# One hybrid decoder layer: another order in the mixer, and dense sums that leave PSUM between the halves of the experts

## The chip, the cores and the metric

The kernel runs on one core of a Trainium2 chip. The metric is the device time of one execution in microseconds; the time of a kernel is the median of its executions. Before the change three executions took 3759.36, 3754.88 and 3768.76 us, so the median is 3759.36.

## The reference, cut to what matters

One layer, `h <- LN(alpha*h + f(h))` three times, over 1024 positions of width 1024, all float32:

```python
# 1. mixer: one projection of h, then two groups of heads side by side
#    GLA: 4 heads, gated linear attention with a decay per channel
scores = einsum('bhtd,bhsd,bhtsd->bhts', qi, ki, decay)
o = scores @ v + (q * exp(b)) @ state;   state = exp(b_last) * state + k_end^T @ v
#    SSD (Mamba-2): 16 heads of width 64, causal convolution, chunked scan with a decay per head
y = (cb * lmat) @ xdt + exp(a_cum) * (c @ h_prev) + d_skip * xs
h = LN(alpha * h + concat(rms(o) * silu(r), rms(y * silu(z))) @ w_out)
# 2. cross-attention, 4 heads, into 256 memory tokens
# 3. PEER: 8 heads x top-16 of 128 x 128 experts of one neuron each
act = einsum('bthk,btd->bthk', u[expert], h)      # u, v: (16384, 1024)
out = einsum('bthk,bthkd->btd', gates * gelu(act), v[expert])
```

## The kernel before, in words

The 1024 tokens are eight tiles of 128. The program has three stages, one after the other; each engine has its own list of instructions in the order of the code and waits on semaphores.

**First stage** (`project_inputs`). Float32 products are made of three products of rounded parts (high x high, high x low, low x high). x comes in eight blocks of 128x1024. For each, VectorE makes the high part (a cast, line 582) and then the low part (a subtraction, line 584); TensorE takes block after block behind them (`product`, line 416). Meanwhile GpSimd cuts the weights (lines 360 to 395), and ScalarE has nothing to do until its first copy (line 493).

**Mixer** (`mix_tokens`). One body per tile on every engine; in the steady part it is a loop of two tiles. TensorE has four PSUM areas A to D of 128x1024, which all products share (`place`). Per tile, in its order: turn x (X, area A), turn the keys (KB, D), level products of heads 0, 1 and 2 (L0 to L2, each eight products of 128x128), turn y of the tile before (OTb, D), L3, the product CB, turn o of the tile before (OTa, B), the products of keys and v (SN), the products with the state (O, line 962), a quarter of the output projection of the tile before (line 895), the diagonal products YD (line 970), and the rest of the projection with YO and HN between. For each head VectorE masks the level products (line 1217) and GpSimd adds the eight levels up in three halvings (lines 864 and 867), 512, 256 and 128 wide; `att_ready` counts heads. The masked terms of heads 0 and 3 share a buffer (`masked`); those of 1 and 2 stand where xdt and xend come later, so these two products (lines 1222 and 1226) wait for their heads' sums. Then VectorE makes the exponents of the next tile's levels (lines 157 to 160), ScalarE exponentiates them (lines 168 to 171) and the SSD decays (line 1098), VectorE multiplies decay by CB (line 1232), and after the root from ScalarE (line 1081) it scales o and updates the state. The output projection's result goes through the first norm on VectorE at the end of the body.

**Retrieval** (`attend_and_retrieve`). Six tiles are gathered, two are dense. The gathered tiles run through 768 slots, one pick of every token each. In a slot GpSimd gathers a row of u per token (`gather_u`, line 1622) and, 20 slots behind (LAG), a row of v (`gather_v`, line 1639), 128 rows of 4 KB each. VectorE multiplies the u rows by h2 and sums (`dot`, line 2180), ScalarE makes the gelu and spreads the weights (line 1965), TensorE combines four rows of v at a time (`combine`, line 1674). u has a ring of five, v of eight. For the first 384 slots the attention and the choice of picks of the later tiles run between ("fronts"). h2 of the current tile stands in PSUM (`h2_near`, the upper half of `wide`) up to slot 443, and in SBUF after it.

The two dense tiles (256 tokens) go through all 16384 experts, in two halves of 64 blocks of 128. From slot 384 (`DENSE_AT`) to 752 their work is laid out over ticks, and `tick_slot` says at which slot a tick comes. A half begins with the *spread*: the gates of the picks are made into a table of 64 keys by 256 tokens per partition. A group is eight tokens: VectorE makes three operations on one-hot rows (`hots`, lines 2446 to 2450), TensorE eight small products (`choose`, line 1779), ScalarE a copy into the table (`keep_chosen`, line 2050). There are 32 groups, two in a tick, and a tick has four slots (`SPREAD_PACE`). Hot rows and results have two buffers each. The picks are read from PSUM (`picksT_near`) in the first spread and from their copy in SBUF (`picksT`) in the second, since by then `wide` holds the sums. Then come the blocks: the table's part times gelu of `dense_u` (line 1791) weighs the block of v in `dense_v` (line 1808), which adds over all 128 blocks in `wide` (128x2048). u and v of the blocks are streamed by SP, 512 KB each. At the end `norm3_a` adds the sums to h2.

## Time and profile before

| what | value |
|---|---|
| median of three executions | 3759.36 us |
| the profiled execution's own time | 3736.6 us |
| its span | 3734.8 us |
| TensorE busy, loading weights | 80%, 54% |
| VectorE, ScalarE, GpSimd busy | 62%, 28%, 52% |
| granted TensorE clock, mean | 0.871 |
| DMA, mean over the span | 292 GB/s |

The profiled execution is 23 us shorter than the median. "Busy" leaves out waiting, branching and issuing. A wait is put down to the event that came last by the profile. All times in the rows are microseconds from the start of the span unless marked ns. A TensorE operation on float32 shows as two records, so eight products of 128x64 stand as x16, and one `dot` as two records of line 2180, of which only the one named CUSTOM is counted below.

### The profile page before, as it was taken

What the parts mean: (1) busy time and instruction counts of PE and PEld (TensorE: products, weight loads), DVE (VectorE), ACT (ScalarE), POOL (GpSimd) and SP (SyncE); (2) the same over time, 40 slices, a digit from 0 to 9 for tenths busy, and PEclk for the clock granted to TensorE, in tenths of its full rate; (3) what the DMA queues carried; (4) which work ended last, traced back from release to release, by engine and by line L of the source; (5) the groups of instructions that cost most, each with busy time, mean ns of one, the idle gap of its engine ahead of it and who ended that gap; (6) DMA issues with size and microseconds to landing.
All of it is one profiled execution on the core that took longest, in us unless ns stands there. A gap on an engine that the chain in (4) does not pass through costs nothing.

```text
span 3734.8 us, 40729 instructions
## 1 busy us (share of the span) xinstructions
PE 3002.1 (80%) x14124; PEld 2007.9 (54%) x14124; DVE 2320.8 (62%) x4974; ACT 1047.2 (28%) x2819; POOL 1925.6 (52%) x1704
## 2 busy tenths in 40 slices
PE   8999978989998756656665544689999967999995
PEld 5878865555656323323323212467777645777771
DVE  3350047777217777778867767776666687666655
ACT  2320123342213323334233212222323222232222
POOL 2342213232103566666665666566565577656566
PEclk9999988999999877777777755679999976999996
DMA  3322252222345999899998999899999999999998
GB/s 123 121 89 96 90 214 83 82 87 83 124 199 185 361 362 375 335 373 369 345 358 337 370 384 347 324 356 409 409 409 409 409 342 329 405 410 409 409 409 341
DMA packets 312855, 1089.76 MB, mean 292 GB/s; under 512 B 33232, under 2 KB 56400, under 8 KB 309600
## 3 DMA queue, kind: packets, MB, share of 16 engines
q0 software_dynamic: 221184, 805.40, 56.6%
q1 hardware_dynamic: 91488, 282.04, 19.8%
q8 instruction: 100, 1.64, 0.2%
q14 instruction: 83, 0.68, 0.0%
HBM read 1051.07 MB, written 36.24 MB: 291 GB/s over the span
## 4 chain that ended last, share of the span: by engine, by line
DMA 18%; PE 17%; POOL 15%; DVE 8%; issue 8%; another core or an unknown queue 3%; ACT 1%; POOLq 0%; DVEq 0%; ACTq 0%
DMA arena<-in_u_dram,idx 12%; POOL arena L1639 7%; POOL arena L1622 7%; DMA arena<-in_v_dram,idx_v 5%; PE small L1791 4%; PE acc L1674 4%; DVE arena L2180 3%; PE wide L1808 3%; PE small L1779 1%; PE small L1733 1%; PE wide L1716 1%; ACT gelu_v L1949 1%; DVE arena L2448 0%; PE small L1881 0%
## 5 line engine op out<-in xcount | busy, mean ns | idle before, releaser
L1622 POOL DMA_INDIRECT arena<-in_u_dram,idx x768 | 797.1, 1038 | 617.7 <-DVE act_u L2180 230.3
L1639 POOL DMA_INDIRECT arena<-in_v_dram,idx_v x752 | 816.1, 1085 | 517.9 <-PE acc L1674 201.4
L1674 PE MATMUL acc<-arena 128*32 128x512 f32 x3008 | 507.3, 792 | 407.7 <-DMA arena<-in_v_dram,idx_v 317.2
L2180 DVE CUSTOM_DVE_ANT_0 arena<-arena,h 128x1024 f32<-128x1024 f32 x348 | 424.2, 1224 | 381.7 <-DMA arena<-in_u_dram,idx 369.2
L2180 DVE CUSTOM_DVE_ANT_0 arena<-arena,wide 128x1024 f32<-128x1024 f32 x420 | 508.4, 1217 | 192.8 <-DMA arena<-in_u_dram,idx 135.1
L1674 PEld LDWEIGHTS acc<-arena 128*32 128x32 f32 x3008 | 102.8, 130 | 678.7 <-issue 563.6
L1791 PE MATMUL small<-pwq 128*128 128x256 f32 x2048 | 466.2, 381 | 1.1 <-DMA pwq<-in_uT_dram 1.1
L1791 PEld LDWEIGHTS small<-pwq 128*128 128x128 f32 x2048 | 386.3, 190 | 82.8 <-issue 26.6
L1965 ACT ACTIVATE arena<-comb,w_v 128x32 f32<-128x32 f32 x768 | 199.0, 311 | 358.9 <-remote 195.3
L416 PE MATMUL group<-w_nat_high,x_parts 128*128 128x512 f32 x768 | 238.2, 391 | 3.8 <-ACT arena L549 3.8
L1779 PE MATMUL small<-arena 128*128 128x64 f32 x1024 | 182.2, 358 | 64.0 <-DVE arena L2450 50.8
L2058 ACT ACTIVATE arena<-small 128x256 f32<-128x256 f32 x128 | 49.3, 385 | 653.0 <-PE small L1791 584.4
L1779 PEld LDWEIGHTS small<-arena 128*128 128x128 f32 x1024 | 175.6, 269 | 104.4 <-DVE arena L2450 69.6
L895 PE MATMUL mix_bank<-memory_tables,mixT 128*128 128x512 f32 x512 | 224.0, 593 | 0.0
L1949 ACT ACTIVATE gelu_v<-act_u 32x4 f32<-32x4 f32 x768 | 159.4, 208 | 222.1 <-DVE act_u L2180 157.3
L416 PE MATMUL group<-x_parts,arena_rounded 128*128 128x512 f32 x864 | 206.8, 400 | 15.7 <-DVE x_parts L584 15.7
L416 PEld LDWEIGHTS group<-x_parts,arena_rounded 128*128 128x128 f32 x864 | 165.2, 193 | 57.8 <-issue 10.8
L1808 PE MATMUL wide<-arena_rounded 128*128 128x512 f32 x512 | 181.5, 436 | 0.2 <-DVE pwq_rounded L2466 0.2
L157 DVE TENSOR_TENSOR arena<-arena 128x256 f32<-128x256 f32 x56 | 31.6, 564 | 236.7 <-DMA arena<-scanT_dram 236.7
L416 PEld LDWEIGHTS group<-w_nat_high,x_parts 128*128 128x128 f32 x768 | 144.3, 188 | 34.6 <-issue 4.2
L1808 PE MATMUL wide<-pwq_rounded,arena_rounded 128*128 128x512 f32 x512 | 160.2, 394 | 0.0
L1808 PE MATMUL wide<-arena_rounded,tables_rounded 128*128 128x512 f32 x512 | 159.1, 392 | 0.0
(347 smaller groups left out, 4618.3 us busy)
## 6 DMA issues: line engine op xcount, KB each, us to landing
pwq<-in_uT_dram SPq DMA_DIRECT2D x128, 512.0 KB
pwq<-in_v_dram SPq DMA_DIRECT2D x128, 512.0 KB
arena<-in_w_nat_dram SPq DMA_DIRECT2D x6, 2048.0 KB, 8.6
nat_dram<-stage SPq DMA_DIRECT2D x48, 256.0 KB, 2.1
arena<-in_u_dram,idx POOLq DMA_INDIRECT x768
arena<-in_v_dram,idx_v POOLq DMA_INDIRECT x752
scanT_dram<-stage SPq DMA_DIRECT2D x22, 512.0 KB, 2.9
arena<-in_w_tr_dram SPq DMA_DIRECT2D x18, 512.0 KB, 3.8
```

What stands on the lines that cost most here:

```text
L416: last = pe.matmul(to, stationary(p, k), moving(q, k), start=(k == 0 and n == 0), stop=(k == KC - 1 and n == 2))
L895: last = pe.matmul(place["OUT"][:, c * 512:(c + 1) * 512], mixT[:, k, :], w_out[:, k, c * 512:(c + 1) * 512], start=(k == 0), stop=(k == 2 ...
L1622: pool.indirect_dma_start(out=u_ring[:, g % U_RING, :], out_offset=None, in_=peer_u, in_offset=bass.IndirectOffsetOnAxis(ap=idx[:, t % KEP ...
L1639: pool.indirect_dma_start(out=v_row(g), out_offset=None, in_=peer_v, in_offset=bass.IndirectOffsetOnAxis(ap=idx_v[:, t % KEPT, n:n + 1], a ...
L1674: last = pe.matmul(acc[c * QUAD:(c + 1) * QUAD, half * 512:(half + 1) * 512], spread_row(at), v_row(at)[:, half * 512:(half + 1) * 512], s ...
L1779: last = pe.matmul(small[:, at:at + HALF_KEYS], hot2[:, q % 2, j, :], hot1[:, q % 2, j, :], start=True, stop=True)
L1791: last = pe.matmul(small[:, at:at + DT], uT_ring[:, i % STREAM, k, :], dense_hT[:, k, :], start=(k == 0), stop=(k == KC - 1))
L1808: last = pe.matmul(wide[:, at:at + 512], w, v[:, c * 512:(c + 1) * 512], start=(i == 0 and n == 0), stop=(i == NKEYS - 1 and n == 2))
L1949: last = act.activation(gelu_v[r * QUAD:(r + 1) * QUAD, h % 2, :].rearrange("p (b c) -> p b c", c=SIDE)[:, :, c], act_u[c * QUAD:(c + 1) * ...
L1965: act.activation(spread_row(g), comb[:, :], ACT.Copy, scale=w_v[:, h % 2, j:j + 1]).then_inc(diag_ready, 1)
L2058: act.activation(gelu_d[:, i % WEIGHED, :], small[:, i % 2 * 512:i % 2 * 512 + DT], ACT.Gelu).then_inc(gelu_d_done, 1)
L2180: dve.tensor_tensor_reduce(out=row, in0=row, in1=against, scale=1.0, scalar=0.0, op0=ALU.mult, op1=ALU.add, accum_out=act_u[:, (n // TOPK) ...
```

## The change

- The high parts of x are cast by ScalarE (new semaphore `x_cut`); VectorE keeps the subtractions.
- In the mixer's body TensorE turns y of the tile before (OTb) right behind X, does L0 to L2, and only then turns the keys (KB); SN comes ahead of the turning of o (OTa). ScalarE scales the turned y first, makes the first eight decays, copies the keys, makes the other eight decays, and makes the exponentials of the next tile behind the root for o. VectorE sums the levels of head 3 itself, with one reduction; xdt and xend both come ahead of the exponents and wait for all four heads.
- A tick of the spread has one group and two slots; TensorE chooses a group one tick behind its hot rows, ScalarE keeps it one tick behind that.
- h2 of the dense tiles is turned at slot 361 (`TURN_AT`), the picks at 384 (`PICKS_AT`); ticks begin at slot 386.
- Each half of the experts has sums of its own in `wide`. Between the halves (slot 569) ScalarE copies the first sums into four pieces of SBUF (`empty_wide`), then puts the picks and h2 back into PSUM; groups from the fourth on (`FROM_SBUF`) and the dots of slots 577 to 627 (`BACK_AT`, `BACK_END`) read them there. `norm3_a` adds the pieces.

```diff
-GROUP_TICKS = GROUPS // 2
+GROUP_TICKS = GROUPS
-SPREAD_PACE = 4
+SPREAD_PACE = 2
@@ first stage, ScalarE
-                act.wait_ge(x_split, 2 * KC)
+                for k in range(KC):
+                    act.wait_ge(x_loaded[k], 16)
+                    act.activation(x_h[:, k, :], x_raw[k], ACT.Copy).then_inc(x_cut, 1)
+                act.wait_ge(x_split, KC)
@@ first stage, VectorE
-                    dve.tensor_copy(x_h[:, k, :], x_raw[k]).then_inc(x_split, 1)
-                    dve.wait_ge(x_split, 2 * k + 1)
+                    dve.wait_ge(x_cut, k + 1)
@@ mixer, TensorE
                     if not first(t):
+                        pe.wait_ge(read["HN"], t)
+                        turned(t - 1, "OTb")
                         pe.wait_ge(levels_ready, t)
-                        pe.wait_ge(read["HN"], t)
-                    (five turns into KB)
-                    if not first(t):
                         pe.wait_ge(read["OUT"], t)
                         levels(t, 0)
...
-                    pe.wait_ge(read["KB"], t + 1)
                     if not first(t):
-                        turned(t - 1, "OTb")
+                        pe.wait_ge(read["OTb"], t)
+                    (five turns into KB)
                     pe.wait_ge(read["L0"], t + 1)
                     levels(t, 3)
...
-                    if not first(t):
-                        pe.wait_ge(read["L3"], t + 1)
-                        turned(t - 1, "OTa")
-                        pe.wait_ge(read["OTb"], t)
+                    pe.wait_ge(read["KB"], t + 1)
                     (products into SN)
+                    if not first(t):
+                        pe.wait_ge(read["L3"], t + 1)
+                        turned(t - 1, "OTa")
@@ mixer, VectorE
+                    dve.wait_ge(read[f"L{SUMMED}"], t + 1)
+                    dve.tensor_reduce(att[:, SUMMED, :], level_terms[SUMMED].rearrange("p (l u) -> p u l", u=P),
+                                      AX, ALU.add).then_inc(att_ready, 1)
                     dve.wait_ge(read["X"], t + 1)
-                    dve.wait_ge(att_ready, GLA_BLOCKS * t + 2)
+                    dve.wait_ge(att_ready, GLA_BLOCKS * (t + 1))
                     dve.tensor_tensor(heads(xdt[:, :], 64), heads(xs[:, :], 64), each(1, 64), ALU.mult)
+                    dve.tensor_tensor(heads(xend[:, :], 64), heads(xs[:, :], 64), each(4, 64), ALU.mult)
                     if not final(t):
                         exponents(t + 1)
-                    dve.wait_ge(att_ready, GLA_BLOCKS * t + 3)
-                    dve.tensor_tensor(heads(xend[:, :], 64), heads(xs[:, :], 64), each(4, 64), ALU.mult)
@@ retrieval
+        PICKS_AT = FRONTS_AT + (TILES - 2) * SPAN + STAGE_SLOTS + CHUNK_SLOTS + 1
+        FROM_SBUF = 3
+        TURN_AT = PICKS_AT - CHUNK_SLOTS // 2
+        DENSE_AT = PICKS_AT + 2
+        BACK_AT = tick_slot(HALF_TICKS) + NEAR_AT
+        BACK_END = tick_slot(HALF_TICKS + GROUP_TICKS + 3) - 4
@@ retrieval, TensorE
-                                                 start=(i == 0 and n == 0), stop=(i == NKEYS - 1 and n == 2))
+                                                 start=(i % HALF_KEYS == 0 and n == 0),
+                                                 stop=(i % HALF_KEYS == HALF_KEYS - 1 and n == 2))
-                    if r < GROUP_TICKS:
-                        for q in (2 * r, 2 * r + 1):
-                            choose(b, q)
+                    if 1 <= r <= GROUP_TICKS:
+                        choose(b, r - 1)
@@ retrieval, ScalarE
+                def empty_wide(t):
+                    act.wait_ge(vb_used, HALF_KEYS)
+                    for n, to in enumerate(held):
+                        last = act.activation(to, wide[:, n * HALF_D:(n + 1) * HALF_D], ACT.Copy)
+                    last.then_inc(part_kept, 1)
+                    act.wait_ge(part_kept, 1)
+                    act.activation(picksT_near, picksT, ACT.Copy).then_inc(picksT_ready, 1)
+                    act.wait_ge(h2_loaded, 16 * t)
+                    act.activation(h2_near, h2[:, t % 2, :], ACT.Copy).then_inc(h2_near_ready, 1)
@@ retrieval, VectorE
-                    picks = picksT_near if b == 0 else picksT
+                    picks = picksT if b == 1 and q < FROM_SBUF else picksT_near
+                    if parts:
+                        dve.wait_ge(part_kept, 2)
+                        for n, part in enumerate(parts):
+                            half = y3[:, n * HALF_D:(n + 1) * HALF_D]
+                            last = dve.tensor_tensor(half, half, part, ALU.add)
-                        for q in (2 * r, 2 * r + 1):
-                            hots(b, q)
+                        hots(b, r)
```

## Rows read from the trace of the kernel before

**Rows 1.** The page, part 1: busy us, share of the span, instructions.

```profile
PE 3002.1 (80%) x14124; PEld 2007.9 (54%) x14124; DVE 2320.8 (62%) x4974; ACT 1047.2 (28%) x2819; POOL 1925.6 (52%) x1704
```

**Rows 2.** Stretch, length; busy us of PE, PEld, DVE, ACT, POOL; clock; DMA share, GB/s.

```profile
509.00:925.00 416.00, 350.39 (x1503) 226.57 (x1502) 294.83 (x465) 144.91 (x368) 136.10 (x99) 0.92 0.33 115
...
2301.00:2498.00 197.00, 142.82 (x778) 101.01 (x774) 152.33 (x230) 50.94 (x160) 119.99 (x125) 0.67 0.91 332
2498.00:2982.00 484.00, 464.67 (x2292) 349.18 (x2288) 302.60 (x518) 142.48 (x386) 294.25 (x251) 0.99 1.03 408
2982.00:3183.00 201.00, 151.35 (x802) 105.58 (x798) 154.80 (x233) 47.12 (x158) 156.68 (x125) 0.68 0.94 339
```

**Rows 3.** Groups by line and shape, 0 to 480 us: busy us, mean ns.

```profile
L584 DVE TENSOR_TENSOR x_parts<-arena,x_parts 128x1024 fp32r<-128x1024 f32 x6 | 10.3, 1720 | 0.2
...
L584 DVE TENSOR_TENSOR x_parts<-stage,x_parts 128x1024 fp32r<-128x1024 f32 x2 | 4.5, 2235 | 0.1
...
L521 ACT ACTIVATE arena<-arena 128x1024 f32<-128x1024 f32 x4 | 4.2, 1062 | 0.0
```

**Rows 4.** Timeline, opening: start us, us, engine, operation, [idle before it, releaser].

```profile
5.94 0.69 DVE L582 CAST x_parts<-arena 128x1024 fp32r<-128x1024 f32 x1 [4.90 <-DMA arena<-in_xT_dram]
...
27.23 8.61 PE L416 MATMUL group<-x_parts,arena_rounded 128*128 128x512 f32 x27 [0.21 <-DVE x_parts L584]
```

**Rows 5.** Timeline of TensorE in one tile of the mixer.

```profile
745.98 1.04 PE L916 MATMUL mix_bank<-ident,xsb 128*128 128x128 f32 x8
...
758.54 1.09 PE L883 MATMUL mix_bank<-ident,o_sb 128*128 128x128 f32 x8 [1.47 <-DVE arena L1217]
...
765.94 1.22 PE L962 MATMUL mix_bank<-gla_state,arena 128*128 128x256 f32 x2 [4.58 <-POOL arena L867]
...
777.95 3.68 PE L970 MATMUL mix_bank<-arena 128*128 128x64 f32 x32
```

**Rows 6.** Timeline of VectorE in the same tile.

```profile
759.82 2.27 DVE L1222 TENSOR_TENSOR arena<-arena,scal 128x1024 f32<-128x1024 f32 x1 [1.33 <-POOL arena L867]
765.15 0.43 DVE L157 TENSOR_TENSOR arena<-arena 128x256 f32<-128x256 f32 x1 [3.06 <-DMA arena<-scanT_dram]
...
772.43 1.22 DVE L1226 TENSOR_TENSOR arena<-arena,scal 128x1024 f32<-128x1024 f32 x1
773.56 2.34 DVE L1232 TENSOR_TENSOR arena<-arena,mix_bank 128x1024 f32<-128x1024 f32 x2
779.96 0.18 DVE L1237 RECIPROCAL arena<-arena 128x4 f32<-128x4 f32 x1 [4.05 <-ACT arena L1081]
```

**Rows 7.** Timeline of ScalarE in the same tile.

```profile
763.16 4.78 ACT L1098 ACTIVATE arena<-arena,scal 128x128 f32<-128x128 f32 x16
772.54 3.19 ACT L168 ACTIVATE arena<-arena 128x3584 f32<-128x3584 f32 x1 [4.60 <-DVE arena L160]
...
778.33 1.28 ACT L1081 ACT_TABLE_LOAD   x1
```

**Rows 8.** Timeline of GpSimd in the same tile, last steps of two sums.

```profile
762.75 0.45 POOL L867 TENSOR_TENSOR arena<-arena 128x128 f32<-128x128 f32 x1
...
765.30 0.58 POOL L867 TENSOR_TENSOR arena<-arena 128x128 f32<-128x128 f32 x1
```

**Rows 9.** Busy times by stretch, behind TensorE's wait in that tile.

```profile
766.00:769.00 3.00, 3.00 (x7) 2.46 (x8) 3.00 (x5) 1.94 (x7) 1.90 (x1) 0.50 0.00 0
```

**Rows 10.** Groups by line, first spread, 2301 to 2498 us.

```profile
L1779 PE MATMUL small<-arena 128*128 128x64 f32 x512 | 92.2, 360 | 36.9 <-DVE arena L2450 23.9 <-issue 12.9
...
L1639 POOL DMA_INDIRECT arena<-in_v_dram,idx_v x62 | 59.8, 965 | 47.2 <-PE acc L1674 18.0 <-issue 15.6 <-remote 13.6
...
L2446 DVE TENSOR_TENSOR arena<-iota,wide 128x512 f32<-128x512 f32 x32 | 21.8, 682 | 16.1 <-ACT arena L2043 8.2 <-remote 7.9
```

**Rows 11.** Groups by line, second spread, 2982 to 3183 us.

```profile
L1622 POOL DMA_INDIRECT arena<-in_u_dram,idx x62 | 80.1, 1292 | 21.2 <-issue 18.3 <-DVE act_u L2180 2.9
...
L1639 POOL DMA_INDIRECT arena<-in_v_dram,idx_v x63 | 77.1, 1223 | 24.7 <-issue 17.4 <-PE acc L1674 7.3
```

89 lines of the change are left out of this document (58 added, 31 removed).

## The prediction

> **What bounds the kernel now.** I read the page first: TensorE is busy for 80% of the span, VectorE for 62% [rows 1], but that is a mean over stages with different limits. The table of windows splits them [rows 2]. There the reader is to see three kinds of stretch. In the mixer (509 to 925 us) nothing is full: TensorE works 350 of 416 us, DMA 33%. In the two dense streams (2498 to 2982 and the like of it from 3183) DMA moves 408 GB/s, its highest rate anywhere, and everything else follows it. In the two spreads (2301 to 2498 and 2982 to 3183) the same gathers run on at only 332 and 339 GB/s, so DMA has room. The change touches the first kind, the third, and the opening microseconds; the dense streams are left to their bytes. As the stages follow one another on the same queues, what one of them gives back goes through to the end.
>
> **Part 1, the cut of x (start).** VectorE makes high and low parts in turn: the first cast starts at 5.94, the last subtraction lets TensorE go at 27.23 [rows 4]. The eight subtractions take 10.3 + 4.5 = 14.8 us [rows 3]; the rest of 21.3 us is casts. With the casts on ScalarE (1.06 us each, from a ScalarE operation of that size from SBUF to SBUF [rows 3]; it is idle until its first copy) only the subtractions stay in a row. The first waits for cast and a table load, about 7.2; 7.2 + 14.8 = 22.0. Saved: 27.2 - 22.0 = 5 us if no x arrives later than that; bounds 2 (subtractions slower beside GpSimd's casts, or x late) and 6.5 (all casts gone). I take 4.
>
> **Part 2, the mixer.** One tile in the middle: TensorE starts the turns of x at 745.98 (P) and idles twice that I can shorten, 1.47 before the turns of o and 4.58 before the state products, for GpSimd's last sum of level terms [rows 5]. GpSimd sums four heads in a row; the third is done at 762.75 + 0.45 = 763.20, the fourth at 765.30 + 0.58 = 765.88, and TensorE goes at 765.94 [rows 5, 8]. The change gives the fourth to VectorE as one reduction of 128x1024. No row has this shape reduced with a stride. VectorE's operations over 128x1024 take 1.22 us, or 2.27 beside GpSimd [rows 6]; either end is over before 763.2, since the fourth mask is done at 758.5 (the product at 759.82 follows it after a wait of 1.3). So the products start at 763.2 instead of 765.94: 2.7 us earlier, 3.5 if GpSimd's third sum is no longer held up by the product at 759.82, which now comes after it. The 1.47 us are filled in part by the v products, moved ahead; they now wait for the copy of the turned keys, which stands behind the turns of y and eight of the sixteen exponentials (half of 4.78 [rows 7]), about 1 us of idleness. Both gaps lie ahead of the same 763.2, so they aren't added.
> What is late next is VectorE. xdt and xend both stand before the exponents now and wait for all four sums: 763.3 + 2.27 + 1.22, then the exponents (765.15 to 772.43, 7.3 us, of which some 1.7 is one piece beside GpSimd, that need not recur), then the product with CB, 2.34 [rows 6]. That is ready at 774.7 to 776.4, against 775.9 now. TensorE needs 12.0 us from the state products to this point (765.94 to 777.95), so it would be there at 775.2 [rows 5]. So a tile gains 2 to 3.5 us. The clock can add to it: after the 4.58 us gap the granted clock was 0.50, the lower level of 1.2 GHz, for the next 3 us [rows 9]; a shorter gap may spare that, up to 2.4 us a tile, where VectorE allows. Seven tiles at 2.8 make 20, and the first one, whose next tile waits for VectorE's long tail, some 4: I take 24, bounds 10 and 40.
> ScalarE's long exponential (3.19 us with its small ones 4.6 [rows 7]) now stands behind the root for o. VectorE's wait of 4.05 us for this root [rows 6] goes, and its products with the levels need the exponentials only some 3.5 us later (two groups of 1.66), so they end together. A slip of a microsecond here costs nothing, since at the end of a tile VectorE waits for the output projection anyway.
> By the Trainium skill (ScalarE: Activation LUTs, "Table sets: the hidden batching unit") exponentials are to be done together and roots together; the new order alternates them and pays two more table loads a tile. The trace has such a load at 1.28 us [rows 7]; if both lay on the path this part would give 24 - 8 x 2.6 = 3 us. I hold that against it as a bound, since ScalarE waits more than it works in the mixer [rows 2].
>
> **Part 3, the spreads.** The floor is DMA: 197 x (1 - 332/408) = 37 us to be had in the first, 201 x (1 - 339/408) = 34 in the second [rows 2].
> First spread. Now two groups of eight tokens come every four slots: VectorE makes both, TensorE waits for them in the same slot (23.9 us in all [rows 10]) and then holds up the combining behind them, so that GpSimd's gathers of v sit idle 18.0 us for TensorE and 13.6 more [rows 10]. Also VectorE waits 8.2 us at the head, for the turning of h2 and the picks and ScalarE's copies, and 7.9 once for an earlier choice. With one group every two slots, chosen one tick later, TensorE finds its operands ready; and h2 is turned 23 slots ahead, so that at the head only six transposes and a copy stand between. GpSimd's own work is 120.0 us busy and some 33 of issuing in 197; the 44 left are waits [rows 2, 10]. I halve them (22), less for the norm of a tile that falls in this stretch as before: 18. Bounds 0 and 37.
> Second spread. GpSimd is the bound here: 156.7 us busy and 35.7 of issuing in 201 [rows 2, 11]. A gather costs 1.29 and 1.22 us, against 0.97 in the first spread [rows 10, 11]; the difference between the two is what VectorE reads: picks and h2 in SBUF here, in PSUM there. With 51 of some 64 slots now reading PSUM, 102 gathers save 0.29 us each, 30 us of GpSimd; but then the waits of the first spread (half of 44) show, 8 of which are there already. 30 - 14 = 16, bounds 0 and 34.
> By the Trainium skill (SBUF, State Buffer, "Who interferes with whom") a VectorE instruction with two SBUF inputs contends with a GpSimd instruction that reads SBUF, as an exclusive lock; by this the 0.29 us would vanish in full, as the first spread's row has it.
> New work: TensorE's sums leave PSUM in four ScalarE copies of 128x512, with one of the picks (128x768), one of h2 (128x1024), and a seventh 32 ticks later. At 1.06 us for 128x1024 [rows 3] the six make some 4 us on ScalarE at slot 569, behind the last value block of the first half. Queued behind it there are the spreads of weights, on which TensorE's combining waits; LAG holds them 20 slots ahead, and ScalarE works only 47 of 201 us [rows 2]. I put it at 0, bounds 0 and 5. Four additions of 128x512 in the norms of the last slots, half of 1.22 each [rows 6] and a little more: VectorE has room there, 0 (bound 3).
>
> **Sum.** 4 + 24 + 18 + 16 = 62 us. The profiled execution took 3736.6 us (span 3734.8), 23 less than the median of 3759.36; it gives 3675, and from the median 3759.4 - 62 = 3697.
>
> **Rivals.**
> A. *The spreads give nothing* (2 in 10): bursts were only shifted, and the latency from dot to next gather sets the pace. For it: both spreads run at the same pace (197 us for 61 slots, 201 for 64: 3.2 and 3.1) though their gathers differ by a quarter. Against it: VectorE's and TensorE's waits on each other. Time: 3759 - 28 = 3731.
> B. *The spreads fall to the DMA floor* (1.5 in 10): every wait was burstiness. 71 + 28 = 99: 3660. For it: GpSimd alone would need only 153 us of 197.
> C. *The lag turns against it, slower* (0.5 in 10): a group's hot rows use one of two buffers and wait for the choice two groups back, which TensorE now reaches only one tick (two slots) before. If TensorE is more than two slots behind VectorE, each group waits, dots stand behind it, and rows of u come free late: a pace of 3.6 us a slot instead of 3.15 costs 0.45 x 125 = 56 us, over the 28 gained: 3787. It decides from 3.4 us a slot. For it: the one wait of 7.9 us was of this kind. Against it: elsewhere TensorE waits for VectorE, not the reverse.
> D. *The mixer gives nothing* (1 in 10): VectorE's longer row before CB (776.4 or later), or the table loads. 4 + 34: 3721.
> My own case has 5 in 10, own range 3675 to 3718.
>
> **Chances.** About 0.5% (19 us) is what can be told from no change. A ends 28 below, near enough to the bound that some of it reads as the same; C is nearly all of slower. Faster 0.85, same 0.11, slower 0.04. Range 3655 to 3737: it takes in B, A and D, and leaves C and mishaps of two parts at once.
>
> **What would show it.** TensorE's row of the state products should lose most of its 4.6 us wait and the tile its 59 to 60 us period for some 56 to 57; the second release of x about 22; gathers in the second spread at 0.97 us; both spreads at 2.8 to 2.9 us a slot, at 360 GB/s or more. I am wrong in the mixer if the diagonal products wait for VectorE for over 1 us, and in the spreads if slots stay at 3.1 while the gathers are short.

## The result, and the profile after

The change took 3721.40 us (median of 4 runs, 3718.18 to 3725.97) against 3758.99 for the kernel before, measured with it (4 runs): ratio 0.9897 [0.9875, 0.9919], some 39 us less. The forecast was 62 less, 3697. The direction and the mixer's mechanism held; the two spreads gave nothing here that can be told from zero. In later sets of runs, in which the kernel before took 3621 to 3623 us and not 3741 to 3759, the same change gave 84 us, and there the spreads did pay. Most of this document is about that difference.

The profile after, part 1 and part 4 (the chain that ended last); the clock was 0.873, the span 3724.1:

```profile
PE 2976.0 (80%) x14124; PEld 1982.6 (53%) x14124; DVE 2308.3 (62%) x4978; ACT 1076.3 (29%) x2848; POOL 1872.3 (50%) x1680
...
PE 19%; DMA 14%; DVE 13%; POOL 10%; issue 8%; another core or an unknown queue 5%; ACT 2%; SPq 0%; POOLq 0%; DVEq 0%; ACTq 0%
```

GpSimd has 53 us less to do than in [rows 1], and the span is only 11 us shorter. (The profiled execution of before was 23 us under its median, so this pair of spans understates the change; the stages below are compared with a second profile of before as well.)

**The opening.** Timeline, columns as in [rows 4]:

```profile
5.37 1.06 ACT L500 ACTIVATE x_parts<-arena 128x1024 fp32r<-128x1024 f32 x1 [3.34 <-DMA arena<-in_xT_dram]
...
6.54 7.31 DVE L586 TENSOR_TENSOR x_parts<-arena,x_parts 128x1024 fp32r<-128x1024 f32 x4 [5.50 <-ACT x_parts L500]
...
13.77 2.35 DVE L586 TENSOR_TENSOR x_parts<-stage,x_parts 128x1024 fp32r<-128x1024 f32 x2
...
16.04 3.19 DVE L586 TENSOR_TENSOR x_parts<-arena,x_parts 128x1024 fp32r<-128x1024 f32 x2
...
19.29 6.42 PE L416 MATMUL group<-x_parts,arena_rounded 128*128 128x512 f32 x27 [0.70 <-DVE x_parts L586]
```

The last release of TensorE is at 19.29, not 27.23 [rows 4]: 8 us earlier. The forecast had 22.0, and 6.5 us as the most that this could give.

**A tile of the mixer.** TensorE, then VectorE, then ScalarE, columns as in [rows 5]; the last fence is the kernel before, at the start of the tile that follows the one of [rows 5]:

```profile
727.20 1.04 PE L919 MATMUL mix_bank<-ident,xsb 128*128 128x128 f32 x8
...
743.65 0.70 PE L964 MATMUL mix_bank<-gla_state,arena 128*128 128x256 f32 x2 [2.57 <-POOL arena L870]
...
755.76 3.68 PE L972 MATMUL mix_bank<-arena 128*128 128x64 f32 x32
...
782.90 1.04 PE L919 MATMUL mix_bank<-ident,xsb 128*128 128x128 f32 x8
```

```profile
739.74 1.96 DVE L1225 TENSOR_REDUCE arena<-arena 128x128 f32<-128x1024 f32 x1
743.63 1.23 DVE L1229 TENSOR_TENSOR arena<-arena,scal 128x1024 f32<-128x1024 f32 x1 [1.93 <-POOL arena L870]
744.77 2.92 DVE L1230 TENSOR_TENSOR arena<-arena,scal 128x1024 f32<-128x1024 f32 x1
...
752.91 2.34 DVE L1238 TENSOR_TENSOR arena<-arena,mix_bank 128x1024 f32<-128x1024 f32 x2
```

```profile
733.73 1.28 ACT L1102 ACT_TABLE_LOAD   x1
...
752.29 1.28 ACT L168 ACT_TABLE_LOAD   x1
```

```profile
805.09 1.04 PE L916 MATMUL mix_bank<-ident,xsb 128*128 128x128 f32 x8
```

Count from the turns of x (P). The state products start at P + 16.45, before at P + 19.96 [rows 5]: 3.5 us earlier. The products behind CB start at P + 28.56 instead of P + 31.97, 3.4 earlier; VectorE's product with CB is over at 752.91 + 2.34 = 755.25, half a microsecond before TensorE comes at 755.76, so VectorE isn't the next wait. The next tile starts at P + 55.7; before, the tile of [rows 5] was followed by the next at 805.09, P + 59.1.

**The spreads.** Busy time by stretch, columns as in [rows 2]; both kernels are cut at the same dots (slots 384 to 448, and 577 to 633), first before, then after:

```profile
2301.00:2507.00 206.00, 151.82 (x820) 107.09 (x813) 157.68 (x240) 53.28 (x165) 126.40 (x130) 0.68 0.91 334
3010.00:3186.00 176.00, 133.68 (x697) 93.74 (x697) 132.38 (x203) 40.21 (x132) 139.86 (x113) 0.67 0.93 332
```

```profile
2278.00:2485.00 207.00, 138.47 (x762) 89.88 (x758) 154.35 (x235) 49.07 (x163) 124.73 (x128) 0.66 0.90 329
2988.00:3175.00 187.00, 123.20 (x710) 83.85 (x709) 131.46 (x205) 41.37 (x138) 107.75 (x113) 0.69 0.88 327
```

206 to 207 us, and 176 to 187. In the second GpSimd is busy for 32 us less and the stretch is 11 us longer. What stands there instead, by groups of lines in 2988 to 3175 (busy, mean ns, idle before it and its releaser):

```profile
L1640 POOL DMA_INDIRECT arena<-in_u_dram,idx x57 | 54.7, 960 | 48.6 <-DVE act_u L2228 32.2 <-issue 16.5
L1657 POOL DMA_INDIRECT arena<-in_v_dram,idx_v x56 | 53.2, 950 | 25.2 <-issue 15.2 <-remote 9.3 <-PE acc L1692 0.6
L1692 PE MATMUL acc<-arena 128*32 128x512 f32 x224 | 42.9, 907 | 47.7 <-ACT arena L1988 42.3 <-DMA arena<-in_v_dram,idx_v 5.3
...
L2501 DVE TENSOR_TENSOR arena<-iota,wide 128x512 f32<-128x512 f32 x27 | 18.5, 684 | 45.0 <-remote 45.0
```

and of the same hot rows in the first spread, 2278 to 2485:

```profile
L2501 DVE TENSOR_TENSOR arena<-iota,wide 128x512 f32<-128x512 f32 x32 | 21.9, 684 | 49.7 <-remote 49.7
```

The gathers did fall, from 1292 and 1223 ns [rows 11] to 960 and 950, as forecast. But the hot rows (L2501) wait 45.0 us in the second spread, GpSimd waits 32.2 us for the dots behind them, and the combining (L1692) 42.3 us for ScalarE. The hot rows wait on one thing only (but for the picks at the first groups), the choice two groups back. It is the place that rival C names; the releaser "remote" says that the profile finds no instruction that ended when the wait did.

**What the wait is.** Timeline of after around one of them:

```profile
3033.47 2.00 PE L1800 MATMUL small<-arena 128*128 128x64 f32 x16
...
3037.76 3.37 PE L1800 MATMUL small<-arena 128*128 128x64 f32 x16 [2.30 <-DVE arena L2505]
3046.30 0.60 ACT L2089 ACTIVATE memory_tables<-small 128x512 f32<-128x512 f32 x1 [6.83 <-remote]
3046.30 0.69 DVE L2501 TENSOR_TENSOR arena<-iota,wide 128x512 f32<-128x512 f32 x1 [6.31 <-remote]
...
3047.22 0.59 ACT L2089 ACTIVATE memory_tables<-small 128x512 f32<-128x512 f32 x1
3047.37 1.08 PE L1692 MATMUL acc<-arena 128*32 128x512 f32 x4 [6.23 <-ACT arena L1988]
...
3050.13 0.94 POOL L1640 DMA_INDIRECT arena<-in_u_dram,idx  x1 [5.98 <-DVE act_u L2228]
```

Counted from 0 over the kernel, the matmuls at 3033.47 are choice 43 and those at 3037.76 choice 44. ScalarE's copy of choice 43 and VectorE's hot rows 45 both wait for the signal of choice 43, and for nothing else. By its records choice 43 ended at 3035.47; both waiters start together at 3046.30, 10.8 us later. ScalarE's spreads of weights are queued behind its copy, and TensorE's combining waits for them. GpSimd's next gather comes at 3050.13, after 5.98 us without one, for the dot behind those hot rows. So TensorE isn't late by its records: its signal is. It isn't a record that is missing either, since all 64 choices stand complete in the trace, 16 records each. And the copy of choice 44 at 3047.22 had no wait at all before it. In all fourteen traces the ends of two choices, by their records, stand at least 1.79 us apart. So if choice 44 had ended by 3047.22, choice 43 had by 3045.43, and its signal reached the waiters at least 0.9 us after its work was done, even if the matmuls ran later than their records say.

### The profile page after: what moved, and what is told of

The parts are those of the page before. It is cut to its first block, busy times and chain, and to the rows that moved or that the text cites. A ratio compares the mean times of both kernels' runs of the same rounds, so it can differ in the third digit from the quotient of the medians.

```text
span 3724.1 us, 40775 instructions
## 1 busy us (share of the span) xinstructions
PE 2976.0 (80%) x14124; PEld 1982.6 (53%) x14124; DVE 2308.3 (62%) x4978; ACT 1076.3 (29%) x2848; POOL 1872.3 (50%) x1680
## 4 chain that ended last, share of the span: by engine, by line
PE 19%; DMA 14%; DVE 13%; POOL 10%; issue 8%; another core or an unknown queue 5%; ACT 2%; SPq 0%; POOLq 0%; DVEq 0%; ACTq 0%
DMA arena<-in_u_dram,idx 7%; DMA arena<-in_v_dram,idx_v 6%; PE small L1812 6%; DVE arena L2228 5%; POOL arena L1657 5%; POOL arena L1640 5%; PE wide L1829 4%; PE acc L1692 4%; PE small L1751 2%; DVE arena L2503 1%; DVE arena L2501 1%; DVE arena L2505 1%; ACT gelu_v L1972 1%; PE wide L1715 0%
## 5 line engine op out<-in xcount | busy, mean ns | idle before, releaser
L1640 POOL DMA_INDIRECT arena<-in_u_dram,idx x768 | 788.1, 1026 | 661.4 <-DVE act_u L2228 272.6
L1657 POOL DMA_INDIRECT arena<-in_v_dram,idx_v x752 | 803.1, 1068 | 519.2 <-issue 204.7
L1692 PE MATMUL acc<-arena 128*32 128x512 f32 x3008 | 509.1, 788 | 471.3 <-DMA arena<-in_v_dram,idx_v 268.3
L2228 DVE CUSTOM_DVE_ANT_0 arena<-arena,wide 128x1024 f32<-128x1024 f32 x472 | 569.5, 1217 | 167.3 <-DMA arena<-in_u_dram,idx 130.7
L2228 DVE CUSTOM_DVE_ANT_0 arena<-arena,h 128x1024 f32<-128x1024 f32 x296 | 359.8, 1224 | 267.4 <-DMA arena<-in_u_dram,idx 253.2
L1692 PEld LDWEIGHTS acc<-arena 128*32 128x32 f32 x3008 | 102.4, 130 | 743.1 <-issue 561.3
L1800 PEld LDWEIGHTS small<-arena 128*128 128x128 f32 x1024 | 158.6, 243 | 92.1 <-issue 61.8
L1800 PE MATMUL small<-arena 128*128 128x64 f32 x1024 | 168.5, 331 | 42.7 <-DVE arena L2505 25.6
L2521 DVE TENSOR_TENSOR pwq_rounded<-pwq,arena_rounded 128x1024 fp32r<-128x1024 f32 x128 | 155.9, 1218 | 5.4 <-ACT arena_rounded L2109 2.7
```

The costliest lines, as they stand in the source:

```text
L1640: pool.indirect_dma_start(out=u_ring[:, g % U_RING, :], out_offset=None, in_=peer_u, in_offset=bass.IndirectOffsetOnAxis(ap=idx[:, t % KEP ...
L1657: pool.indirect_dma_start(out=v_row(g), out_offset=None, in_=peer_v, in_offset=bass.IndirectOffsetOnAxis(ap=idx_v[:, t % KEPT, n:n + 1], a ...
L1692: last = pe.matmul(acc[c * QUAD:(c + 1) * QUAD, half * 512:(half + 1) * 512], spread_row(at), v_row(at)[:, half * 512:(half + 1) * 512], s ...
L1800: last = pe.matmul(small[:, at:at + HALF_KEYS], hot2[:, q % 2, j, :], hot1[:, q % 2, j, :], start=True, stop=True)
L2228: dve.tensor_tensor_reduce(out=row, in0=row, in1=against, scale=1.0, scalar=0.0, op0=ALU.mult, op1=ALU.add, accum_out=act_u[:, (n // TOPK) ...
L2521: dve.tensor_tensor(vb_l[:, i % STREAM, :], vb_ring[:, i % STREAM, :], vb_h[:, i % 2, :].bitcast(F32), ALU.subtract).then_inc(vb_l_ready, 1)
```

## The experiments

Twelve runs, in three sets, e1 to e4, e5 to e8 and e9 to e12; each ratio is to the kernel before, run in the same set. The row "the change" is the first measurement (kernel before 3758.99 us), which belongs to none of the three. The kernel before took 3740.51 us (23 runs) in the first set, 3621.17 (9) in the second, 3623.46 (9) in the third. The stage columns are from the profiled execution: the start of the first turn of x, the mixer from there to its last product, and the two spreads between the same dots as above. "Gather" is the mean of GpSimd's gathers from the dot of slot 577 to that of slot 628, the part in which the change reads PSUM. Below, "where signals are late" is the first measurement and the first set, and "where they are prompt" the second and the third; e9 shows the difference.

```
kernel                    ratio [95% interval]    start mixer 384-448 577-633 gather
before (first profile)    -                       518.3 571.4  206.0   175.8  1269 ns
e1 before again           0.9988 [0.9967,1.0008]  519.9 572.3  206.1   177.9  1277
e2 mixer only             0.9898 [0.9877,0.9920]  509.8 542.8  208.1   176.3  1268
e3 retrieval only         0.9994 [0.9977,1.0011]  520.7 572.1  206.7   175.6   936
the change                0.9897 [0.9875,0.9919]  509.4 544.6  207.5   187.2   940
e4 no return              0.9917 [0.9893,0.9941]  510.4 542.1  197.2   179.0  1276
- second set (e5 to e8)
e5 no lag                 0.9782 [0.9768,0.9795]  510.3 543.0  175.0   151.7   937
e6 pairs                  0.9799 [0.9785,0.9812]  509.8 542.9  175.0   153.5   937
e7 slot lag               0.9759 [0.9745,0.9772]  511.1 543.2  173.2   149.7   937
e8 pool sums, old spreads 0.9948 [0.9934,0.9961]  509.9 563.0  192.0   174.4  1235
- third set (e9 to e12)
e9 the change again       0.9769 [0.9756,0.9782]  511.0 544.9  173.7   144.9   939
e10 slot lag again        0.9751 [0.9737,0.9764]  511.6 542.9  170.8   145.6   937
e11 slot lag, no return   0.9851 [0.9836,0.9866]  509.4 542.8  171.9   182.9  1319
e12 no lag again          0.9781 [0.9767,0.9794]  509.3 544.8  175.4   150.7   937
```

**e1: the kernel before, once more.** No edit.

> The kernel before, unchanged, for a second trace and as a measure of noise. Ratio 1.000, within 0.3%. The first profiled execution (3736.6 us) was 22 us under the median of its kernel; if the second is near the median (3755 to 3760), its stages against those of the first show where an execution gains or loses such 20 us, and whether the saving by stage (start and mixer 37 us less, retrieval 27 us more in the trace after) is to be read with that correction. Theory 1: the stages up to the retrieval are the same within 1 us in every execution, and the difference lies in the retrieval, whose gathers depend on memory. Theory 2: it lies in the mixer too.

0.9988 [0.9967, 1.0008]: no difference, as it must be. Its profile (span 3738.0) is a truer picture of before than the first, and its stages differ from it by 2 us at most in the columns above. That is two profiles; others with the same code in a stretch differ by more. The change's first spread took 207.5 us and e4's, whose code there is the same, 197.2; up to slot 384 the gathered slots took the change 1156 us, e2 1140 and e4 1139. So where signals are late, one profile tells no stage of gathers apart by 10 us; the ratios are better evidence.

**e2: start and mixer alone**, the retrieval as before:

```
-GROUP_TICKS = GROUPS
+GROUP_TICKS = GROUPS // 2
-SPREAD_PACE = 2
+SPREAD_PACE = 4
 (all from retrieval_constants on: the text of the kernel before)
```

> The kernel before with the change's first stage and mixer alone; the retrieval is that of before. Theory 1 (the whole gain is start and mixer, the spreads gave nothing or lost): ratio 0.989 to 0.991, first dot some 37 us earlier, time 3718 to 3724. Theory 2 (start and mixer gave the forecast 28 us and the retrieval the rest, about 10): ratio 0.9925, 3731.

0.9898, the whole change's 0.9897. In stages, against the mean of the two profiles of before: start 9 us less, mixer 29 less; 38 together, and 0.0102 x 3740 = 38.

**e3: the retrieval alone**, start and mixer as before (the counterpart of the edit above).

> The kernel before with the change's retrieval alone; start and mixer are those of before. Theory 1 (the two changes in the spreads cancel or lose): ratio 0.998 to 1.004, second spread 5 to 15 us longer than in the kernel before. Theory 2 (the retrieval gave 10 us or more): ratio 0.995 to 0.997, the spreads shorter by that.

0.9994 [0.9977, 1.0011]: nothing, or by the interval between 9 us less and 4 more. That is rival A's outcome: the gathers are short (936 ns) and yet the pace stays, which is also what A's reason would give, so this run doesn't decide on it; e9 does. The second spread took 175.6 us, no longer than in the kernel before, against the 5 to 15 us more of theory 1, though its retrieval is the change's to the letter. The 187.2 us of the change's profile aren't repeated here, with as many late signals in the whole trace (119 over 2 us late in both, counted as under e9). Waits of its second spread, then those of the change (waiter, releaser: us in all, times, longest):

```profile
ACT memory_tables L2083 <- remote: 87.4, 13, 18.1
DVE arena L2495 <- remote: 31.0, 7, 10.0
```

```profile
ACT memory_tables L2089 <- remote: 93.2, 10, 18.2
DVE arena L2501 <- remote: 45.0, 8, 10.4
```

**e4: the change without the return to PSUM**, so that VectorE reads picks and h2 from SBUF through the whole second spread:

```
-        FROM_SBUF = 3
+        FROM_SBUF = GROUPS
-        BACK_END = tick_slot(HALF_TICKS + GROUP_TICKS + 3) - 4
+        BACK_END = BACK_AT
-                    act.activation(picksT_near, picksT, ACT.Copy).then_inc(picksT_ready, 1)
-                    act.activation(h2_near, h2[:, t % 2, :], ACT.Copy).then_inc(h2_near_ready, 1)
...
+                    if i == HALF_KEYS:
+                        pe.wait_ge(part_kept, 1)
```

> The changed kernel, but picks and h2 are not put back into PSUM: in the second spread all groups read the picks and all dots h2 from SBUF. The first sums still leave PSUM. Theory 1 (VectorE waits for the choice two groups back, GpSimd's gathers are not what bounds the second spread any more): gathers of the second spread rise to 1.2 to 1.3 us, but the spread stays within 5 us of the changed kernel's 210; ratio against before within 0.15% of the changed kernel's. Theory 2 (the return to PSUM is what keeps the second spread from being worse, as the shorter gathers are on the path): the second spread takes 225 us or more and the kernel 15 us more than the changed one.

0.9917 [0.9893, 0.9941] against the change's 0.9897 [0.9875, 0.9919], which is of the first measurement: not to be told apart. Its second spread took 179 us, 8 less than the change's and 3 more than e3's, so neither theory's bound was met; it ran with gathers at 1276 ns and without one wait for "remote"; with gathers of 1.27 us the signals came in time, as in the second spread of before, where no such row stands either.

```profile
2960.00:3139.00 179.00, 129.00 (x712) 86.77 (x712) 134.28 (x205) 42.18 (x139) 142.57 (x115) 0.69 0.93 337
```

The short gathers and the late signals come together here: of the 32 us that GpSimd saves none is left in the time; they reappear as waits.

**e5: no lag** (a group is chosen in the tick in which it is made):

```
-                    if 1 <= r <= GROUP_TICKS:
-                        choose(b, r - 1)
+                    if r < GROUP_TICKS:
+                        choose(b, r)
...
 (ScalarE keeps the group r - 1 in tick r, before it kept r - 2)
```

> The changed kernel with TensorE choosing a group in the tick of its hot rows (one group, two slots), ScalarE keeping it one tick later. Theory 1 (the lag of a tick is what makes VectorE wait for the choice two groups back, 43 us in the second spread, and takes back what the shorter gathers give): those waits fall under 15 us, the second spread (slots 577 to 633) goes from 187 to 165 us or less, the first likewise by 10 or more; ratio against before some 0.984 to 0.986. Theory 2 (TensorE's wait for hot rows in the same tick simply takes their place): both spreads within 5 us of the changed kernel's, ratio 0.989 to 0.991.

**e6: pairs** (two groups every four slots as before, with the return to PSUM):

```
-GROUP_TICKS = GROUPS
+GROUP_TICKS = GROUPS // 2
-SPREAD_PACE = 2
+SPREAD_PACE = 4
...
+                        for q in (2 * r, 2 * r + 1):
+                            choose(b, q)
...
 (and so two groups in hots and keep_chosen)
```

> The changed kernel with two groups in a tick of four slots, chosen in the same tick, as before; picks and h2 go back to PSUM in the second spread. So it has the return to PSUM without the other order. Theory 1 (the order with the lag is at fault, short gathers help by themselves): slots 577 to 633 take 165 us or less, against 176 to 178 in the kernel before; ratio 0.986. Theory 2 (once gathers are short, something else holds the same pace of 3.1 us, as it did in the first spread of the kernel before): 172 to 178 us, ratio 0.989 to 0.990.

**e7: slot lag** (a group is chosen one slot after it is made, half of the change's lag):

```
-                    if 1 <= r <= GROUP_TICKS:
-                        choose(b, r - 1)
...
+                        for tick in ticks_at(slot - 1):
+                            if tick % HALF_TICKS < GROUP_TICKS:
+                                choose(tick // HALF_TICKS, tick % HALF_TICKS)
                         for tick in ticks_at(slot):
...
 (ScalarE as in e5)
```

> The changed kernel with TensorE choosing a group one slot behind its hot rows instead of one tick (two slots), ScalarE keeping it in the next tick. Theory 1: as the choice two groups back is done a slot earlier and TensorE need not wait for fresh hot rows, both spreads are shorter than with either whole lag: slots 577 to 633 at 160 us, first spread at 180, ratio 0.983. Theory 2: between the two neighbours, ratio 0.989 to 0.991.

All three gave 0.976 to 0.980, and at first this looked as if each had cured the wait. It can't be read so: in this set the kernel before was itself 119 us faster. That is why the changed kernel was run again, in e9. The expectations were built on the times of the first set, so by their numbers none of the three is decided.

**e8: GpSimd sums all four heads** (start and mixer of the change with the retrieval of before, VectorE's reduction taken out):

```
-        SUMMED = GLA_BLOCKS - 1
+        SUMMED = GLA_BLOCKS
-                    dve.tensor_reduce(att[:, SUMMED, :], level_terms[SUMMED].rearrange("p (l u) -> p u l", u=P),
-                                      AX, ALU.add).then_inc(att_ready, 1)
```

> The kernel with start and mixer of the change and the retrieval of before (ratio 0.9898), but GpSimd sums the levels of all four heads again, as before; VectorE's reduction is left out. Theory 1 (the sum of the fourth head, on VectorE, is what lets TensorE go earlier): the state products start 2.5 us later in each tile, the period goes from 55.5 to 58 or more, mixer 542 to 562 us, ratio 0.995. Theory 2 (the order and the early root carry the mixer's gain): the period stays under 56.5, mixer under 550.

Theory 1 holds, close to its numbers: mixer 563.0 us against 542.8 with the reduction, ratio 0.9948. So the fourth sum carries 20 of the 29 us, everything else in the new order the other 9. TensorE in a tile of it:

```profile
735.79 1.04 PE L919 MATMUL mix_bank<-ident,xsb 128*128 128x128 f32 x8
...
754.76 1.08 PE L964 MATMUL mix_bank<-gla_state,arena 128*128 128x256 f32 x2 [5.09 <-POOL arena L870]
...
794.02 1.04 PE L919 MATMUL mix_bank<-ident,xsb 128*128 128x128 f32 x8
```

The wait of before is back (5.09 us, before 4.58 [rows 5]), the state products stand at P + 18.97, and the period is 58.2 us, between the change's 55.7 and before's 59.1. e8 also shows the old spreads in a set in which before takes 3621 us: 192.0 and 174.4 us. And e6 of the same set differs from it in the retrieval by everything but the new order of the groups: it has the early turning of h2, the ticks that begin two slots later and the return to PSUM, with two groups in four slots, chosen at once, as before. First spread of e8, then of e6:

```profile
2183.00:2375.00 192.00, 143.36 (x815) 104.09 (x808) 157.70 (x242) 54.03 (x169) 125.35 (x130) 0.70 0.94 358
```

```profile
2162.00:2337.00 175.00, 130.26 (x778) 90.56 (x774) 155.59 (x238) 50.85 (x165) 125.11 (x129) 0.74 1.00 389
```

So 17 us of the first spread and 21 of the second come without the new order. About half of the 17 is the head: the slots 384 to 391 took 30.8 us in e8, with VectorE's wait of 7.5 us for ScalarE's copies of what was turned in it, and 22.0 in e6. What brings the rest isn't shown.

**e9: the changed kernel again**, no edit.

> The changed kernel itself, for a comparison on one chip with e10 to e12: the executions of e5 to e8 took 3621 us for the kernel before, against 3740 to 3759 earlier, and their gathers moved 398 GB/s where the others moved 355, so ratios of the two sets can't be set against each other. Theory 1 (the lag of a tick costs on every chip): hot rows wait 30 us or more for an earlier choice in slots 577 to 628, and the second spread is 10 us or more longer than in e10. Theory 2 (the lag cost only where gathers are slow): on a chip with fast gathers the changed kernel is within 5 us of e10 and e12; ratio 0.977.

0.9769 [0.9756, 0.9782], 84 us, as theory 2 has it. No variant of e5 to e7 had cured anything: the change itself is as good where they are. (The second and the third set can be compared: e5 and e12, the same kernel, took 3543.23 and 3542.34 us, e7 and e10 3533.50 and 3533.98.) Against e6, the new order gives 1 us in the first spread and 9 in the second, 11 in the medians (3550.60 and 3539.26). Its spreads, and its chain:

```profile
2166.00:2340.00 174.00, 133.13 (x766) 86.96 (x761) 156.05 (x237) 50.01 (x164) 127.44 (x130) 0.71 1.01 395
2844.00:2988.00 144.00, 105.60 (x702) 66.64 (x705) 131.70 (x203) 41.54 (x138) 106.67 (x112) 0.85 1.03 408
```

```profile
DMA 23%; PE 20%; DVE 11%; POOL 10%; issue 5%; ACT 2%; SPq 0%; POOLq 0%; DVEq 0%; ACTq 0%
```

The share of "another core or an unknown queue" is gone from the chain. It is 3% to 5% in before, e1 to e4 and the change, and in none of e5 to e12. The same signals in e9:

```profile
2893.30 2.89 PE L1800 MATMUL small<-arena 128*128 128x64 f32 x24
2895.34 0.60 ACT L2089 ACTIVATE memory_tables<-small 128x512 f32<-128x512 f32 x1 [6.02 <-PE small L1800]
2895.34 0.69 DVE L2501 TENSOR_TENSOR arena<-iota,wide 128x512 f32<-128x512 f32 x1 [0.44 <-PE small L1800]
```

TensorE's row holds matmuls of two choices; the first of them ends at 2895.30, and both waiters start 0.04 us later. Over whole traces I took each idle time of over 1 us on ScalarE, VectorE and GpSimd that waits for one semaphore last raised by TensorE, and the time from the record's end to the waiter's start. Over 2 us late were 90 in before, 80 in e1 and 119 in the change, 424, 389 and 674 us in sum (two waiters for one signal count twice), and 93 to 119 in e2 to e4. All of the change's lie where rows are gathered outside the dense streams: 77 before slot 384, 22 in the first spread and 20 in the second. In each of e5 to e12 there is none. Of the waits of ScalarE and VectorE for each other and of GpSimd for them, three were that late in e1 and four in the change. DMA over the second spread (GB/s in forty slices), first the change (3000 to 3170), then e9 (2850 to 2980):

```profile
GB/s 365 318 353 418 411 283 98 310 358 416 411 138 214 299 399 417 339 349 403 418 128 198 327 395 316 138 306 349 401 328 401 416 408 221 150 303 386 374 292 291
```

```profile
GB/s 401 407 410 412 408 411 408 410 408 410 412 403 407 412 408 407 412 407 407 410 408 410 410 410 410 408 406 411 410 410 410 407 411 406 408 411 410 407 412 411
```

The change runs at the full rate and then falls into holes; one of them is the 5.98 us without a gather before 3050.13, above, while a signal is out. e9 stands on the DMA floor of the dense streams [rows 2] throughout. That is rival B's end for the second spread; the first stays at 395 GB/s, 2.7 us a slot.

**e10: slot lag again**, the edit of e7.

> The changed kernel with TensorE choosing a group one slot behind its hot rows (as e7). Theory 1: 20 to 35 us faster than e9 in the same set, both spreads shorter, no waits of hot rows. Theory 2: within 5 us of e9. In both it is the fastest of the four, or level with e12.

0.9751 [0.9737, 0.9764]: 5 us under e9, where theory 1 had 20 to 35. The first spread is 3 us shorter, the second 1 us longer.

**e11: slot lag without the return to PSUM**, the edits of e7 and e4 together.

> As e10, but picks and h2 are not put back into PSUM in the second spread. Theory 1 (once no lag stands in the way, the contention of VectorE's two SBUF inputs with GpSimd's gathers bounds the second spread): slots 577 to 633 take 172 to 178 us against 150 to 165 in e10, and the kernel 15 to 25 us more. Theory 2 (the return buys nothing): within 5 us of e10.

0.9851 against e10's 0.9751: the return is worth 36 us (3569.55 - 3533.98), and 37 in its stage, more than theory 1 had (15 to 25). Second spread of e11, then of e10:

```profile
2838.00:3021.00 183.00, 126.67 (x714) 83.76 (x713) 134.42 (x206) 41.71 (x138) 148.56 (x114) 0.70 0.91 322
```

```profile
2837.00:2983.00 146.00, 118.77 (x713) 79.20 (x713) 133.02 (x206) 41.38 (x138) 106.90 (x112) 0.75 1.02 401
```

and the gathers of e11:

```profile
L1640 POOL DMA_INDIRECT arena<-in_u_dram,idx x57 | 79.7, 1398 | 17.4 <-issue 17.4
L1657 POOL DMA_INDIRECT arena<-in_v_dram,idx_v x57 | 70.9, 1243 | 17.4 <-issue 17.4
```

GpSimd has 148.6 us of work and 34.8 of issuing in 183: it is the bound, with no other wait of its gathers. With the return it has 42 us less, and DMA becomes the bound at 401 GB/s. The same operand move is worth 37 us here and nothing that shows where signals are late (e4 against the change).

**e12: no lag again**, the edit of e5.

> The changed kernel with TensorE choosing a group in the tick of its hot rows (as e5). Theory 1 (both whole lags lose something, this one TensorE's wait for hot rows): 3 to 12 us slower than e10, 15 or more faster than e9. Theory 2: level with e9.

0.9781 [0.9767, 0.9794], e9 0.9769 [0.9756, 0.9782], e10 0.9751 [0.9737, 0.9764]. Taking the lag out costs 3 us in the medians (e12 against e9), with overlapping intervals, so theory 2 holds; a lag of a slot is 8 us better than none here and 10 in the second set (e7 against e5), where the intervals overlap by a little and here just don't. The best version I have is the slot lag, 3533.98 us against the change's 3539.26: the fastest of both its sets, but not shown to be better than the change.

## Why the prediction was right or wrong

**The direction and the size.** Faster by 39 us in the first measurement, with 62 forecast; 84 in the third set. The forecast lies between two settings, in one of which the spreads gave nothing and in the other 48 us, with 34 forecast. That the first measurement, 3721, is inside the range and not far from the forecast is in part luck: parts 1 and 2 gave 10 us more than their terms (38 for 28), and the spreads 34 less (0 for 34). Rival D's time, 3721, is the measured one, and its story the reverse of what happened: it had nothing from the mixer and all from the spreads.

**Part 1, the start: mechanism right, too small.** Forecast 4, measured 8 at the last release and 9 at the first turn of x. The term that was too small is the subtractions, which I kept at the 14.8 us of [rows 3]. From 6.54 to 19.23 they take 12.7 us. Most take 1.21 us after the change and 1.22 before; the others, three before (2.2 to 3.2 us) and four after (1.6 to 2.4), all stand beside work of GpSimd's, and after the change they lose less by it. ScalarE's first cast was there at 6.43, and I had allowed 7.2. The 8 us are over the upper bound of 6.5 too, since I had let the casts go and no subtraction get shorter.

**Part 2, the mixer: right, a little small.** Forecast 24, measured 27 to 30. I gave a tile 2 to 3.5 us and took 2.8; it gained 3.5 and 3.4 at the two marks and 3.4 in its period. The guess on the reduction was fair (1.96 us, with 1.22 and 2.27 as bounds), and e8 shows that it is the main piece. The wait of 4.58 us became 2.57, where I had said that most of it would go: TensorE comes to it earlier. The clock, which I thought could add up to 2.4 us a tile, gave nothing: in the 3 us behind the wait the granted clock was 0.62 (743.65 to 746.65), before 0.50 [rows 9], and the eight state products, from the first to the projection behind them, took 5.24 us, before 5.14. Rival D is out, as VectorE's row ended 0.5 us before it was wanted.
By the Trainium skill (ScalarE: Activation LUTs, "Table sets: the hidden batching unit") exponentials belong together and roots together, since each switch costs a load. The tile has two more loads at 1.28 us, and it gained all the same; ScalarE was busy for 178 of the 416 us from 509 to 925 and isn't the bound there.

**Part 3, first spread: the step failed in the first measurement, and where the number held the step gave little of it.** Forecast 18: measured -1 (206.1 in e1, 207.5 in the change) where signals are late, with up to 9 by e4's profile, and 18 (192.0 in e8, 173.7 in e9) where they are prompt. That the 18 is met there is luck: e6, without one group every two slots and without the lag, has 17 of it, half of them at the head, where I had the early turning of h2 right. The step that failed is "TensorE finds its operands ready", or rather what I built on it: that waits between engines are as long as the work that they wait for. In the first measurement TensorE's signals came late on their own, and the new order has one such signal in each loop of two slots, with only two buffers to absorb it: VectorE waited 49.7 us for it in the first spread, against 7.9 before [rows 10]. I had that 7.9 in hand, with "remote" as its releaser, and the 13.6 of GpSimd beside it; I read both as TensorE's being behind, and took half of them as something that a better order removes.

**Second spread: the term was 16; measured -11 to +2 where signals are late, and 30 in the third set.** The -9 to -11 are the change's profile against the two of before; e3, the same retrieval, has 0 to +2, and its ratio of 0.9994 says the same of both spreads together. Its first half, that VectorE's reads from PSUM shorten the gathers, was right in size in both: 1.27 to 0.94 us, 32 us of GpSimd. By the Trainium skill (SBUF — State Buffer, "Who interferes with whom") a VectorE instruction with two inputs in SBUF contends with a GpSimd instruction that reads SBUF, for a shared port that one of them holds alone. The traces agree on the contention, with gathers of 936 to 940 ns with PSUM and 1235 to 1319 without, and e10 against e11 differ in this alone; how long one holds the port isn't shown. The "waits of the first spread", which I let take 14 us of it, took all of the 30 where signals are late. Where they are prompt it took 9 of them in e6 (21 left), and nothing with the new order.

**The rivals.** A's number for the spreads (0) held in the first measurement. Its reason, a fixed latency from dot to gather, doesn't: e9's slots ran at 2.7 and 2.6 us with the same code. B held in the third set for the second spread (408 GB/s, 30 us of 34) and for the first by half (395 GB/s, 18 us of 37). C's place was right, and its mechanism not: TensorE isn't two slots behind by its records, and where signals are prompt e12 is no faster than e9 for having no lag. In the change's second spread the waits cost 9 to 11 us net at most, and nothing in e3's, not 56.

**What stays open.** Why TensorE's signals reach their waiters late in some sets no run here tells. The runs of the first set and of the second are recorded with the same chip number (1), those of the third with another (10). If the number names one chip, the same chip had late signals in one set and none in the next, some 20 minutes later, and it is a condition and not a chip; the first measurement has no number. That late signals go with short gathers close together is seen, not its cause: in the second spread of before, e1, e2 and e4, with gathers of 1.27 us, there is none, and in the dense streams and behind them 0 to 3 a trace. Whether the matmuls also ran late, unseen by the records, is open too; that at least one signal came after its work is shown above. Nor is it shown that the late signals make up the whole of the 119 to 138 us between the settings, for the rate of the gathers differs too (355 and 397 GB/s, below) and either may follow from the other. And no lag, pairs and slot lag weren't run in a set with late signals, so whether one of them keeps the spreads' gain there isn't known.

## What to carry to other kernels

A wait whose releaser is "remote" in a one-core kernel need not be slack that a better order removes; here it wasn't. Compare the record's end of whatever raises that semaphore with the waiter's start, and count the signals in the loop before you shorten it. Before two variants are compared, look at the time of the unchanged kernel beside each; the ratio of a variant from one set and of the original from another can't be set against each other. When a term comes out as forecast, look for a run that has the gain without the step it was put down to; e6 is one here. And an operand moved from SBUF to PSUM under GpSimd's gathers was worth its 0.3 us a gather only where GpSimd was the bound; read GpSimd's busy time plus its issuing against the stretch first.

## What the runs showed of the hardware

- The same kernel took 3759, 3741, 3621 and 3623 us in four sets. In the fourteen traces the second dense stream (slots 633 to 752) took 464 to 470 us, whatever the set, and the mixer of the change 544.6 and 544.9. The difference lies where rows are gathered outside the streams: up to slot 384 the gathered slots took 1139 to 1156 us in the traces with late signals and 1040 to 1042 in the others. Over 1500 to 1900 us of the change and of e9:

```profile
1500.00:1900.00 400.00, 252.15 (x1236) 125.89 (x1240) 313.41 (x929) 142.45 (x455) 258.84 (x262) 0.76 0.95 355
```

```profile
1500.00:1900.00 400.00, 263.92 (x1378) 129.18 (x1377) 348.53 (x1026) 150.22 (x472) 286.69 (x293) 0.80 1.01 397
```

- A sum over eight strided parts, 128x128 from 128x1024, took VectorE 1.96 us, against 1.22 for a product over 128x1024.
- VectorE's product at 744.77 took 2.92 us, where its neighbour of the same shape took 1.23; GpSimd was at an addition of 128x1024 from 743.74 on, for 2.87 us.
